# One-hot rows of the first key: one VectorE operation a block, weighed on ScalarE, and 12 pairs of rows beside the blocks

## What is computed

```python
s = jnp.einsum('thpd,pkd->thpk', q, sk)              # two halves of a key
sv, si = lax.top_k(s, PEER_TOPK)
...
ts, tp = lax.top_k(cand, PEER_TOPK)                  # 16 of the 256 sums, per head
e = jnp.take_along_axis(cidx, tp, axis=-1)           # expert = first key * 128 + second key
g = jax.nn.softmax(ts, axis=-1)
a = jax.nn.gelu(jnp.einsum('thkd,td->thk', u_tab[e], hb))
return jnp.einsum('thk,thkd->td', g * a, v_tab[e])
```

## Time and profile before

| | |
|---|---|
| median of 3 runs | 2184.49 us (2183.03 to 2186.46) |
| profiled execution | 2185.89 us, its span 2184.1 us |
| busy over the span | PE 98%, DVE 80%, ACT 28%, POOL 39% |
| block stage | from 1392 us to 1604 us of the span |
| down stage on PE | from 1645 us to 2173 us of the span |

### The profile page before, as it was taken

One profiled execution on the slowest core, in us unless ns is written; L12 is line 12 of the kernel. 1 busy time (PEld: TensorE's weight loads), 2 busy tenths in 40 slices (PEclk: granted clock), 3 DMA queues, 4 the chain that ended last, 5 costly groups with the idle time before them and its releaser, 6 DMA issues.

```text
span 2184.1 us, 31103 instructions
## 1 busy us (share of the span) xinstructions
PE 2139.8 (98%) x10569; PEld 1706.0 (78%) x10569; DVE 1746.6 (80%) x3270; ACT 619.3 (28%) x1197; POOL 860.8 (39%) x606
## 2 busy tenths in 40 slices
PE   6999999999999999999999999999999999999997
PEld 6999989999998985655565565677767888888886
DVE  2577586676765286898989979999969999999998
ACT  4212213132223111121211211233324444443434
POOL 4222122223333004475685675411145444444440
PEclk9999999999999999999999999999999999999999
DMA  5999999989983458999999999888999999999995
GB/s 191 300 329 308 300 299 330 333 299 326 305 287 136 137 195 336 336 372 412 397 410 412 383 412 412 299 290 298 301 340 411 414 414 413 414 414 414 414 415 202
DMA packets 312713, 732.28 MB, mean 335 GB/s; under 512 B 30208, under 2 KB 162048, under 8 KB 312576
## 3 DMA queue, kind: packets, MB, share of 16 engines
q1 hardware_dynamic: 188352, 436.52, 55.4%
q0 software_dynamic: 73728, 268.47, 31.3%
q10 hardware_dynamic: 50496, 25.59, 3.9%
HBM read 602.46 MB, written 128.00 MB: 334 GB/s over the span
## 4 chain that ended last, share of the span: by engine, by line
PE 61%; DMA 16%; DVE 14%; issue 4%; SPq 2%; ACT 1%; POOL 0%; DVEq 0%; ACTq 0%
PE ps L1833 29%; DMA b<-acts 12%; PE ps L1793 6%; PE ps L1596 6%; PE ps L1595 6%; PE ps L1594 6%; DMA b<-in_u_t 4%; PE ps L1848 4%; DVE b L1463 3%; DVE b L1509 2%; DVE b L1446 1%; DVE b L1515 1%; DVE b L1500 1%; SPq L527 1%; DVE b L1103 1%
## 5 line engine op out<-in xcount | busy, mean ns | idle before, releaser
L1833 PE MATMUL ps<-b,b 128*128 128x384 f32 x2048 | 665.6, 486 | 0.0
L732 POOL DMA_INDIRECT b<-u_rows,b x256 | 362.6, 1416 | 677.9 <-DVE b L1446 489.1
L1833 PEld LDWEIGHTS ps<-b,b 128*128 128x128 f32 x2048 | 386.8, 190 | 263.4
L695 POOL TENSOR_TENSOR b<-b,b 128x1024 fp32r<-128x1024 f32 x80 | 196.8, 2463 | 468.6 <-ACT b L745 464.0
L1463 DVE SCALAR_TENSOR_TENSOR b<-b,b,b 128x1024 f32<-128x1024 f32 x256 | 330.8, 1292 | 49.0 <-ACT b L966 32.6
L1594 PE MATMUL ps<-b,b 128*128 128x320 f32 x1152 | 364.5, 316 | 0.0
L1595 PE MATMUL ps<-b,b 128*128 128x320 f32 x1152 | 357.0, 310 | 0.0
L1596 PE MATMUL ps<-b,b 128*128 128x320 f32 x1152 | 357.0, 310 | 0.0
L732 POOL DMA_INDIRECT b<-in_peer_v,b x256 | 288.8, 1128 | 118.1 <-issue 76.9
L1446 DVE CUSTOM_DVE_ANT_0 b<-b,b 128x1024 f32<-128x1024 f32 x256 | 312.5, 1221 | 25.3 <-DMA b<-u_rows,b 23.8
L1103 DVE STREAM_TRANSPOSE b<-b 128x1024 f32<-128x1024 f32 x128 | 158.0, 1241 | 186.5 <-DMA b<-in_u_t 178.7
(11 more groups left out here) (164 smaller groups left out, 2414.0 us busy)
## 6 DMA issues: line engine op xcount, KB each, us to landing
b<-in_u_t SPq DMA_DIRECT2D x256, 512.0 KB, 6.5
u_rows<-b SPq DMA_DIRECT2D x512, 128.0 KB, 4.4
b<-in_peer_v SPq DMA_DIRECT2D x128, 512.0 KB, 22.1
b<-in_w_in SPq DMA_DIRECT2D x72, 512.0 KB, 6.4
b<-in_wq SPq DMA_DIRECT2D x48, 512.0 KB, 4.4
gates<-b ACTq DMA_DIRECT2D x12, 2048.0 KB, 8.3
b<-gates SPq DMA_DIRECT2D x32, 768.0 KB, 17.4
acts<-b SPq DMA_DIRECT2D x120, 192.0 KB, 7.9
```

The costliest lines, as they stand in the source:

```text
L695: nc.gpsimd.tensor_tensor(lo[u][:, :], raw[:, u, :], hi[u][:, :].bitcast(F32), ALU.subtract).then_inc(lo_ready, 1)
L732: nc.gpsimd.indirect_dma_start(slots[n % SLOTS][:, :], None, u_rows if kind == "u" else v_rows, bass.IndirectOffsetOnAxis(ap=row_id[:, r_ ...
L1833: last = nc.tensor.matmul(ps[:, up_bank(e), 0:TD], w[:, k * P:(k + 1) * P], h2[:, k, SD:T], start=(k == 0), stop=(k == KT - 1))
```

## The change

VectorE makes the first key's one-hot rows of a block in one operation, unweighed, in the form that `eq2` had already, and signals that alone. ScalarE then multiplies the 8 matrices of the block with their gates in place, one operation for each token, with the gate as a scale of one number per partition. ScalarE does this for the two blocks of tile `e + 1` within its part for tile `e`, ahead of the four `gate_out` of tile `e`. PE waits for that as well before it scatters a block. Beside the blocks stand 12 pairs, one behind every fourth block, and the ScalarE part of them stands at every second up tile; 44 pairs are left for the down stage.

```diff
-BESIDE_HOTS = 8
+BESIDE_HOTS = 12
...
-        return GATE_AT + 3 * i if i < BESIDE_HOTS else GATE_ENDS - 2 + i - BESIDE_HOTS
+        return GATE_AT + 2 * i if i < BESIDE_HOTS else GATE_ENDS - 2 + i - BESIDE_HOTS
...
+            def weigh_onehots(blk_):
+
+                act.wait_ge(first_key_ready, blk_ + 1)
+                for t in range(BLK):
+                    at_ = blk_ * BLK + t
+                    own = ew[:, blk_ % HOTS, t, :]
+                    last = nc.scalar.activation(own, own, ACT.Copy, scale=wT[:, at_:at_ + 1])
+                last.then_inc(onehot_weighed, 1)
...
+                if GATE_AT <= e + 1 < GATE_ENDS:
+                    for blk_ in range(2 * (e + 1 - GATE_AT), 2 * (e + 1 - GATE_AT) + 2):
+                        weigh_onehots(blk_)
                 if GATE_AT <= e < GATE_ENDS:
                     for n in range(4 * (e - GATE_AT), 4 * (e - GATE_AT) + 4):
                         gate_out(n)
...
-                for t in range(BLK):
-                    at_ = blk_ * BLK + t
-                    nc.vector.tensor_scalar(ew[:, par, t, :], iotaK[:, :], k1T[:, at_:at_ + 1], wT[:, at_:at_ + 1],
-                                            ALU.is_equal, ALU.mult)
+                nc.vector.tensor_tensor(ew[:, par, :, :], keys, each(k1T[:, tok]), ALU.is_equal).then_inc(first_key_ready, 1)
...
-                if blk_ % 6 == 4:
+                if blk_ % 4 == 2:
                     next_pair()
...
             def scatter(blk_):
                 par = blk_ % HOTS
+                pe.wait_ge(onehot_weighed, blk_ + 1)
                 pe.wait_ge(onehot_ready, blk_ + 1)
```

More of the change, by code:

```diff
@@ L451, in build_program @@
         onehot_ready = sem("onehot_ready")
+        first_key_ready = sem("first_key_onehot_ready")
+        onehot_weighed = sem("onehot_weighed")
         onehot_used = sem("onehot_used")
```

## The result

The changed kernel takes 2189.02 us (median of 10 runs, 2185.41 to 2192.64) and the kernel before 2183.42 (10 runs on the same chip, 2182.23 to 2186.46): 5.6 us more, ratio 1.0023 with a 95% interval of 1.0013 to 1.0032. The prediction said 5.7 us more, and slower.

What follows compares the result with a forecast made beforehand. PE was taken as the bound, with at most 5.5 us to win. Repeated waits 5.4 plus start 2.3 minus down stage 2.0 made 5.7 us more, 2190.2 us on the median's scale; range 2184 to 2202, slower given 0.60.

Steps and rivals of the forecast that it cites:

- What bounds the kernel: Whole kernel: PE sets the end; its waits of 0.9 and 2.9 us and the 1.7 tail cap any gain at 5.5.
- The price of a weighing: ScalarE, block stage: one 128-column multiply costs 0.30 us, between 0.193 and 0.39; 384 of them add 115 us.
- The path: Block stage, end of an up tile to first freed bank: 9.20 us against PE's 8.73, so PE waits 0.47.
- The loop on ScalarE: Block stage, one pair's weights to the next pair's: 17.95 us for two tiles against PE's 17.46, 0.49 too long.
- The repeated waits: Block stage, the 11 pairs behind the first: PE waits 0.49 us at each, 5.4 us more.
- The start: First pair of the block stage: PE waits 2.9 us behind up tile 97, 2.3 us more in all.
- The down stage: Four pairs fewer there: late waits go, early ones stay, 2.0 us back, with 0 and 4.6 as ends.
- That the down stage follows VectorE or the DMA engines: Rival: these set PE's pace in the down stage, 19 us come out, 2173 us; chance of faster 0.05.
- That the weighings don't overlap: Rival, ScalarE in the block stage: 0.39 us each, 29 us more, 2215 us; more than 2202 given 0.10.
- That ScalarE keeps ahead: Rival, block stage: weighing at 0.24 us or less, no repeated wait, 2184.8 us; no change given 0.35.
- That the 16 gathers cost nothing in the block stage: Block stage: 16 gathers of 512 KB move in, DMA engines go from 0.88 to nearly 1.0, nothing charged.

Runs made afterwards that it cites:

- fifteen_pairs: The changed kernel with 15 pairs beside the blocks, one behind every third block, weights one to two up tiles ahead, 41 left for the down stage: ratio 0.9971.
- the three runs that cured the order with 12 pairs: The changed kernel with pairs behind both blocks of an up tile, with banks emptied before weighing, or with both: ratios 0.9980, 0.9986 and 0.9980.
- early_gelu: The changed kernel with ScalarE making the weights of the 12 pairs beside the blocks one up tile earlier: ratio 0.9999.
- weigh_alone: The changed kernel with the 8 pairs where the kernel before has them, so only the weighing moved to ScalarE: ratio 1.0011.
- pair_behind: The changed kernel with the 12 pairs behind both blocks of an up tile, not between them: ratio 0.9980.
- half_weighed: The changed kernel with ScalarE weighing only 4 of each block's 8 tokens: ratio 0.9997.
- eight_between: ScalarE weighing with only 8 pairs, each between two blocks of an up tile, its weights made one tile ahead, against the kernel before: ratio 1.0023.
- twelve_alone: The kernel before with 12 pairs placed as in the changed kernel, but its weighed one-hot rows still made on VectorE: ratio 1.0026.

## Why the prediction was right

**What bounds the kernel.** Right. The limit of 5.5 us on any gain came from PE's waits and the tail; the best version here (fifteen_pairs) gained 0.29% or 6.3 us against its own runs of before, the limit within its interval, and its stages give 0.9 + 2.9 + 1.7 = 5.5 us; the three runs that cured the order with 12 pairs gained 3 to 4.4.

**The price of a weighing.** Taken as 0.30 us from the two neighbours; measured, 16 in a row take 4.79 us with 0.394 for one, so (4.79 - 0.394) / 15 = 0.293 from start to start. The line between the rows of 1 and 1024 columns was right within 2%. The Trainium skill ("ScalarE: Activation LUTs", section "What ACT_TABLE_LOAD costs") has figures that give an estimate of 0.293, and the trace agrees with it.

**The path.** Predicted 9.20 us and a wait of 0.47, measured 9.22 and 0.49. The weighings were 0.04 shorter, and the first bank's emptying with its signal to PE 0.06 longer. **The loop on ScalarE**, which I took as the one that counts, had a little room: from 1494.24 to the end of the store's issue at 1511.54, with 0.39 for the next emptying, are 17.7 us, and ScalarE then had 0.34 us to spare until it could begin at 1511.88 (the row's 0.74 counts from the last emptying, with the issue in it). Predicted were 17.95. So it is the path that decides, by the same 0.49; the choice between the two was wrong and changed nothing. The loop isn't harmless: 17.7 is still 0.2 above PE's 17.46, so by this sum PE would have waited a little even if the path had fitted; no run shows that alone.

**The repeated waits.** Predicted 11 x 0.49 = 5.4; from up tile 98 to up tile 120 the stage is 198.4 us long against 192.6, 5.8 more. Each wait also costs 0.09 in the scatter that follows it (1506.52 - 1502.87 = 3.65 against 3.56), so the 11 come to 6.4; 0.44 of the difference goes the other way, for the second wait of before fell into this stretch (1425.97 - 1408.07 = 17.90 for two tiles, not 17.46).

**The start.** The wait behind up tile 97 was predicted as 2.9 us and is 2.73, and PE comes to that scatter 2.4 us late, as predicted. What the step lacked is the clock: the scatter behind the wait took 1.7 us longer, at a granted clock that had fallen (below). With it, and the 0.4 above, the block stage cost 9.9 us and not 7.7.

**The down stage.** Taken as 2.0 us, with 4.6 as the end; measured 2.2 + 1.7 = 3.9. This is the term that was sized too small. The prediction had the pattern right: the two early waits stayed (1.4 us) and the two late ones went (1.5). But these and the tail of 1.7 already make 3.2 by its own rows, and it took 2.0 without a reason for less. The late part went whole, since VectorE with 19 us less to do catches up with PE and waits for it.

So two terms were off by some 2 us each, in opposite directions: the block stage cost 2.2 more than predicted, most of it the clock, and the down stage gave back 1.9 more. That the total came within 0.1 us of the forecast is luck; the path and its 11 waits are not.

**The rivals.** That the down stage follows VectorE or the DMA engines is refuted by fifteen_pairs: VectorE's busy time between 1660 and 2140 us falls from 455.1 in the kernel before to 434.3 us and the DMA share from 1.02 to 0.97, and with these seven pairs fewer the stage is only 2.9 us shorter, where this rival has 19 us for four. That the weighings don't overlap is refuted by the 0.293. That ScalarE keeps ahead was a matter of 0.49 us in 8.73, and early_gelu shows how near it lay. That the 16 gathers cost nothing in the block stage, which the prediction assumed, the stages bear out: 210.1 us in weigh_alone, which has none of them, in pair_behind, which has all 16, and in fifteen_pairs, with 28 more than the kernel before has there.

## What to carry to other kernels

When work moves between engines that run strictly in order, add up the path through the hand-overs, not the busy shares: here both engines had room and PE waited, because a result made behind tile e was placed ahead of work that tile e + 1 needed. An engine's wait costs only what stands behind it in its own order. Of the changed kernel's block stage, moving the pairs by one block took 10.8 us, emptying the banks first 10.2 and making the weights one tile earlier 7.9; leaving out half of the weighing took 7.4. And when an engine beside the bound gets relief, look at the end of the stage for the gain, and at the first hand-over for the loss.

## What the runs showed of the hardware

After PE's wait of 2.73 us in the changed kernel the granted clock was lower for a few microseconds. PE by stretches (length, busy and instructions, clock, DMA share, GB/s):

```profile
1408.00:1412.00 4.00, 1.27 (x10) 1.00 0.99 347
1412.00:1416.00 4.00, 4.00 (x23) 0.57 0.64 222
1416.00:1420.00 4.00, 4.00 (x17) 1.00 0.19 22
```

Between 1413 and 1415 us it was 0.50, the lower of its two levels (1.2 of 2.4 GHz). The same scatter of 32 products then took 5.27 us and not 3.56, in the changed kernel, in half_weighed behind a wait of 2.06 us, and in eight_between behind 2.74. In twelve_alone, behind a wait of 2.21, the granted clock of two stretches of 4 us was 0.83 and 0.74, and the up tile behind it took 6.32 us, not 5.33:

```profile
1409.51 2.77 PE L1848 MATMUL ps<-b,b 128*128 128x128 f32 x16 [2.21 <-DVE b L1485]
1412.07 6.32 PE L1833 MATMUL ps<-b,b 128*128 128x384 f32 x16
```

But in early_gelu the same wait of 2.73 us was followed by a scatter of 3.65 us at full clock, and in the changed kernel itself the wait of 2.51 us before 1393.41 left the clock at 1.00. So a wait of over 2 us on PE can cost nearly as much again, and what decides whether it does stays open: no run here settles it. The repeated waits of 0.5 us left the clock at 1.00.
